# Expert outputs added by one-hot and diagonal products on TensorE, with another order and size of the expert tiles

## What is computed

```python
def hier_moe(h, w_rg, b_rg, w_re, b_re, w_gate, w_up, w_down):
    t = h.reshape(b * s, d)
    p_group = softmax(t @ w_rg + b_rg)
    pg_top, g_top = top_k(p_group, 1)
    p_exp = softmax(einsum('nge,ng->ne', logits_e, g_onehot))
    pe_top, e_top = top_k(p_exp, 2)
    pe_top = pe_top / sum(pe_top)
    combine = one_hot(g) * one_hot(e) * pe_top * pg_top
    for gi in range(4):
        hid = silu(einsum('nd,edf->nef', t, w_gate[gi])) * einsum('nd,edf->nef', t, w_up[gi])
        y = y + einsum('nef,efd->nd', hid * combine[:, gi, :, None], w_down[gi])
# afterwards: x = x + gate(c) * y ; out = rms_norm(x, final_norm)
```

## Time and profile before

| | |
|---|---|
| median of 3 runs | 781.9 us (779.35 to 783.69) |
| the profiled run | 781.9 us, of which the span is 780.0 us |
| busy, share of the span | PE 88%, DVE 41%, ACT 23%, POOL 15% |
| granted TensorE clock, mean | 0.946 of full |
| moved by DMA | 173.62 MB, mean 223 GB/s |

### The profile page before, as it was taken

How to read it: one execution, slowest core, us unless ns; L and a number is a source line. 1 busy time by engine, 2 the same in 40 slices (tenths; PEclk the granted TensorE clock), 3 DMA queues, 4 the chain that set the end, 5 groups by cost and what they waited for, 6 DMA issues and landing times.

```text
span 780.0 us, 9903 instructions
## 1 busy us (share of the span) xinstructions
PE 686.8 (88%) x3851; PEld 401.5 (51%) x3851; DVE 318.2 (41%) x752; ACT 180.0 (23%) x434; POOL 116.7 (15%) x164
## 2 busy tenths in 40 slices
PE   1799899999999999879999985899999999999830
PEld 1674446667666697545654455444444544443210
DVE  3203657856466533786612228350211211202126
ACT  3204215122121121456711141020111211201103
POOL 8700122313032155000000000010000000000030
PEclk9989999999999999899999986999999999999975
DMA  9999003793330300750085047638999999999965
GB/s 332 375 264 364 3 1 108 245 294 109 108 108 1 52 5 7 266 216 2 1 324 108 28 179 280 195 110 349 375 423 413 405 413 409 390 404 410 421 208 201
DMA packets 75475, 173.62 MB, mean 223 GB/s; under 512 B 21954, under 2 KB 38940, under 8 KB 71836
## 3 DMA queue, kind: packets, MB, share of 16 engines
q1 hardware_dynamic: 69520, 157.59, 56.0%
q0 software_dynamic: 2672, 9.44, 3.5%
q10 hardware_dynamic: 3228, 5.84, 2.0%
HBM read 156.59 MB, written 16.26 MB: 222 GB/s over the span
## 4 chain that ended last, share of the span: by engine, by line
PE 76%; DVE 9%; POOL 4%; issue 4%; ACT 3%; DMA 3%; POOLq 0%; ACTq 0%; DVEq 0%
PE ps L1031 14%; PE ps L1153 7%; PE ps L1064 7%; PE ps L2300 7%; PE ps L2267 5%; PE ps L1025 4%; PE ps L1059 2%; PE ps L2378 2%; PE ps L2264 2%; PE ps L2384 2%; DMA expert_rows<-yo 2%; PE ps L2291 2%; POOL lev L1648 2%; PE ps L653 2%; PE ps L2388 2%
## 5 line engine op out<-in xcount | busy, mean ns | idle before, releaser
L1031 PE MATMUL ps<-gu,xgT 128*128 128x512 f32 x256 | 113.0, 600 | 3.6 <-DVE xgT L1110 2.5
L1031 PEld LDWEIGHTS ps<-gu,xgT 128*128 128x128 f32 x256 | 48.6, 192 | 63.2 <-issue 63.2
L2300 PE MATMUL ps<-hT,winr 128*128 128x512 f32 x144 | 72.6, 612 | 0.0
L1540 POOL DMA_INDIRECT xg<-xn_rows,list x15 | 13.9, 928 | 384.7 <-DVE list L1447 185.9
L1153 PE MATMUL ps<-wout,yT 128*128 128x512 f32 x128 | 57.6, 610 | 0.0
L1064 PE MATMUL ps<-dn,hidT 128*128 128x512 f32 x128 | 56.5, 594 | 0.0
L1753 POOL TENSOR_TENSOR cc<-low,lev 128x512 f32<-128x512 f32 x20 | 30.2, 1518 | 129.5 <-DVE low L2087 104.0
L1891 DVE SCALAR_TENSOR_TENSOR acc<-ada,st,acc 128x512 f32<-128x512 f32 x56 | 48.5, 866 | 1.3
L2267 PE MATMUL ps<-hT,wind 128*128 128x512 f32 x96 | 43.4, 605 | 0.0
L1025 PE MATMUL ps<-gu,xgT 128*32 128x256 f32 (+1 forms) x384 | 43.0, 452 | 0.0
L1153 PEld LDWEIGHTS ps<-wout,yT 128*128 128x128 f32 x128 | 24.6, 195 | 30.0 <-issue 30.0
(11 more groups left out here) (433 smaller groups left out, 1046.6 us busy)
## 6 DMA issues: line engine op xcount, KB each, us to landing
dn<-in_w_down SPq DMA_DIRECT2D x16, 2048.0 KB, 23.3
gu<-in_w_gate SPq DMA_DIRECT2D x15, 2048.0 KB, 21.5
gu<-in_w_up SPq DMA_DIRECT2D x15, 2048.0 KB, 26.0
ada<-in_w_ada SPq DMA_DIRECT2D x12, 2048.0 KB, 11.6
expert_rows<-zero SPq DMA_DIRECT2D x12, 512.0 KB, 6.7
expert_rows<-yo ACTq DMA_DIRECT2D x8, 512.0 KB
wout<-in_w_out SPq DMA_DIRECT2D x1, 3072.0 KB, 10.6
x<-in_x SPq DMA_DIRECT2D x2, 1024.0 KB, 6.2
```

What stands on the lines that cost most here:

```text
L1031: ins = nc.tensor.matmul(PS[2 * b + w][:, :], T["xgT"][:, k, :], w_in[:, w, k, :], start=(k == 0), stop=(k == KT - 1))
L2300: ins = t.matmul(bank[:, :], w(k), T["hT"][:, k, :], start=(k == 0), stop=(k == KT - 1))
```

## The change

- Tile sizes are 7 x 128, 5 x 64, 4 x 32, the order is 0, 1, 2, 12, 3, 11, 4, 10, 5, 9, 6, 8, 7, 13, 14, 15, and there are 13 extra tiles.
- Positions 4 and 5 are refilled in quarters too, as the products of positions 1 and 2 go on.
- The last three positions (`on_chip`) are not stored. VectorE writes their 32 rows each to `yc` in SBUF. In the routing it also makes one-hot rows times the weight for them; TensorE turns these at position 4 (`pe_onehot`), ScalarE copies them to `back`. For a token of such an expert the weight of the gathered row is set to zero, and its slot points to a zero row.
- y1 is gathered when the positions up to 11 are stored and G(13) has ended, y2 when position 12 is stored.
- At the end TensorE multiplies y1 and y2 by diagonals of w1 and w2 (`diag1`, `diag2`) and `yc` by `back`, summed in all 8 PSUM banks, 24 products of 128x512 (`pe_back`). VectorE adds the banks to x2.
- Extra tiles stand inside one branch that is not taken when there are none, with a gather and sum of their own.
- The mean and epsilon of two norms move into ScalarE's Sqrt, whose table is loaded ahead of the last norm.

```diff
-SIZES = [128] * 8 + [64] * 4 + [32] * 4
+SIZES = [128] * 7 + [64] * 5 + [32] * 4
+CHIP = 3
...
-                if n == NBUF:
+                if n < 2 * NBUF:
+                    b = n - NBUF
                     for part in range(4):
                         if part < 3:
-                            sp.wait_ge(sem("first_gu_mm"), part + 1)
+                            sp.wait_ge(sem("first_gu_mm"), 3 * b + part + 1)
                         else:
-                            sp.wait_ge(sem("gu_mm"), 1)
+                            sp.wait_ge(sem("gu_mm"), b + 1)
                         ks = slice(2 * part, 2 * part + 2)
                         for w, view in enumerate((wg_v, wu_v)):
-                            sp.dma_start(gu[0][:, w, ks], view[expert[n]][:, ks]).then_inc(sem("gu_in0"), 16)
+                            sp.dma_start(gu[b][:, w, ks], view[expert[n]][:, ks]).then_inc(sem(f"gu_in{b}"), 16)
...
+    def pe_back(pe):
+        pe.wait_ge(sem("routing"), ROUTING["route_i"])
+        pe.wait_ge(sem("exp_out"), 3)
+        pe.wait_ge(sem("diag"), 1)
+        pe.wait_ge(sem("y1_in"), 16 * ST)
+        for i in range(ST):
+            if i == 2:
+                pe.wait_ge(sem("yo_d"), E + 1)
+            for n in range(2):
+                if n:
+                    pe.wait_ge(sem(f"y_in{i}"), 16)
+                for w in range(2):
+                    nc.tensor.matmul(PS[2 * i + w][:, :], T[f"diag{n + 1}"][:, i, :],
+                                     T[f"y{n + 1}"][:, i, w * 512:(w + 1) * 512], start=(n == 0), stop=False)
+            pe.wait_ge(sem("yo_d"), E + 1)
+            for w in range(2):
+                ins = nc.tensor.matmul(PS[2 * i + w][:, :], T["back"][:, i * P:(i + 1) * P],
+                                       T["yc"][:, w * 512:(w + 1) * 512], start=False, stop=True)
+            ins.then_inc(sem("oproj_mm"), 1)
...
+        if on_chip(n):
+            dve.wait_ge(sem("yo_d"), E - CHIP + 1)
+            dve.wait_ge(sem("xg_tr"), E)
+            to = slice(32 * (n - E + CHIP + 1), 32 * (n - E + CHIP + 2))
+            for w in range(4):
+                rows, c = slice(32 * w, 32 * w + 32), slice(256 * w, 256 * w + 256)
+                ins = nc.vector.tensor_tensor(T["yc"][to, c], PS[down_bank(n)][rows, 0:256], T["g2q"][rows, :],
+                                              ALU.mult)
...
         dve_output(dve, E - 1)
+        for i in range(ST):
+            dve.wait_ge(sem("oproj_mm"), ST + i + 1)
+            for w in range(2):
+                x = T["x2"][:, i, w * 512:(w + 1) * 512]
+                ins = v.tensor_tensor(x, PS[2 * i + w][:, :], x, ALU.add)
+            ins.then_inc(sem("x3"), 1)
...
+        extras(dve, n_extra, extra, extra_rows_back)
         dve.wait_ge(sem("fn_in"), 16)
...
-            dve.wait_ge(sem(f"y_in{i}"), 16)
-            v.scalar_tensor_tensor(x, T["y2"][:, i, :], w2[:, i:i + 1], x, ALU.mult, ALU.add).then_inc(sem("x3"), 1)
...
         pool.wait_ge(sem("routing"), ROUTING["slots"])
-        pool.wait_ge(sem("yo_st"), 16 * STORED[E - 1])
+        pool.wait_ge(sem("gu_mm"), E - CHIP + 1)
+        pool.wait_ge(sem("yo_st"), 16 * STORED[E - CHIP - 1])
         for i in range(ST):
             rows_back(0, "y1_in", i)
-        n_extra = extras(pool, extra)
...
-        pool.wait_ge(sem("yo_st"), 16 * STORED[E])
+        pool.wait_ge(sem("yo_st"), 16 * STORED[E - CHIP])
         for i in range(ST):
             rows_back(1, f"y_in{i}", i)
```

More of the change, by code:

```diff
@@ L188, in sbuf_map @@
     o2 = at("r16", o2, [P, ST, E])
+    at("back", o2 + 2 * K, [P, S])
+    at("diag1", o2, [P, ST, P])
     o2 = at("in_row", o2, [P, 2, ST, P])
@@ L1014, in pe_gate_up @@
         w_in = gu[buffer_of(n)]
-        pe.wait_ge(sem(f"gu_in{buffer_of(n)}"), 32 * loads_of(n) + (96 if n >= NBUF and not buffer_of(n) else 0))
+        pe.wait_ge(sem(f"gu_in{buffer_of(n)}"), 32 * loads_of(n) + (96 if n >= NBUF else 0))
         pe.wait_ge(sem("xgT_a"), n + 1)
@@ L1136, in dve_output, with extra_count, extras @@
         ins.then_inc(sem("yo_d"), 1)
-    def extras(eng, body):
+    def extra_count(eng):
         eng.wait_ge(sem("routing"), ROUTING["route_i"])
[L1141 to L1145, removed]
+        return eng.value_load(T["route_i"][0:1, 0:1], min_val=0, max_val=EXTRA)
+    def extras(eng, n_extra, body, last=None):
+        with eng.If(n_extra > 0):
+            for x in range(EXTRA):
+                with eng.If(n_extra > x):
+                    body(x, E + x)
+            if last:
+                last()
     Y_ORDER = (0, 1, 6, 7, 2, 3, 4, 5)
@@ L1252, in extra @@
             pe_down(pe, n)
-        extras(pe, extra)
+        extras(pe, n_extra, extra)
     def act_moe(act):
@@ L1304, in extra @@
             act_hidden(act, n, 0)
+            if n == E:
+                act.wait_ge(sem("yo_zero"), 16 * (EXTRA + 1))
             act_output(act, n)
-        extras(act, extra)
+        extras(act, n_extra, extra, lambda: act.wait_ge(sem("x3"), 2 * ST))
+        a.activation(rden[:, 0:1], one, ACT.Sqrt)
         for i in range(ST):
@@ L1475, in dve_moe @@
         dve.wait_ge(sem("routing"), ROUTING["w12"])
+        slotf, virtual, mine = T["slotf"][:], T["place"][:], T["first"][:]
+        link(v.tensor_scalar(virtual, slotf, 32.0 - CHIP_ROW, None, ALU.add))
+        for n, w in enumerate((w1, w2)):
+            for i in range(ST):
+                ins = v.tensor_scalar(T["in_row"][:, n, i, :], T["row_n"][:], virtual[:, n, i:i + 1], w[:, i:i + 1],
+                                      ALU.is_equal, ALU.mult)
+        link(ins)
+        v.tensor_tensor(T["in_row"][:, 0], T["in_row"][:, 0], T["in_row"][:, 1], ALU.add).then_inc(sem("routing"), 1)
+        link(v.tensor_scalar(mine, slotf, CHIP_ROW - 0.5, None, ALU.is_gt))
+        link(v.scalar_tensor_tensor(virtual, slotf, -float(ZERO_ROW), mine, ALU.add, ALU.mult))
+        link(v.tensor_tensor(slotf, slotf, virtual, ALU.subtract))
+        link(v.tensor_scalar(mine, mine, -1.0, 1.0, ALU.mult, ALU.add))
+        link(v.tensor_tensor(w1, w1, mine[:, 0], ALU.mult))
+        link(v.tensor_tensor(w2, w2, mine[:, 1], ALU.mult))
         swap, move = T["mx"][:], T["mn"][:]
-        link(v.tensor_scalar(t16, order, float(LAST), None, ALU.is_equal))
-        link(v.tensor_tensor(T["s16"][:], T["M1"][:], t16.unsqueeze(1).broadcast_to([P, ST, E]), ALU.mult))
-        link(v.tensor_reduce(swap, T["s16"][:], AX.X, ALU.add))
+        link(v.tensor_scalar(swap, T["slotf"][:, 0, :], MID_ROW - 0.5, None, ALU.is_gt))
         for one_of, two in ((w1, w2), (T["slotf"][:, 0, :], T["slotf"][:, 1, :])):
@@ L1492, in dve_moe @@
         link(v.tensor_scalar(T["rf"][:, 1:1 + EXTRA], T["rf"][:, 1:1 + EXTRA], float(E - 1), None, ALU.min))
-        v.tensor_copy(T["route_i"][:, 0:1 + EXTRA], T["rf"][:, 0:1 + EXTRA]).then_inc(sem("routing"), 1)
+        link(v.tensor_copy(T["route_i"][:, 0:1 + EXTRA], T["rf"][:, 0:1 + EXTRA]))
+        for i in range(ST):
+            ins = v.tensor_scalar(T["diag2"][:, i, :], idf[:], w2[:, i:i + 1], None, ALU.mult)
+        ins.then_inc(sem("routing"), 1)
+        n_extra = extra_count(dve)
         for n in range(1, E):
@@ L1500, in dve_moe @@
                 dve_output(dve, n - 1)
-        dve_output(dve, E - 1)
+            if n == E - 2:
+                v.memset(T["yc"][0:32, :], 0.0)
+            if n == ONEHOT_AT + 1:
+                dve.wait_ge(sem("routing_pe"), ROUTING_PE["list_mm"] + 1)
+                for i in range(ST):
+                    ins = v.tensor_scalar(T["diag1"][:, i, :], idf[:], w1[:, i:i + 1], None, ALU.mult)
+                ins.then_inc(sem("diag"), 1)
+        dve_output(dve, E - 1)
+        for i in range(ST):
+            dve.wait_ge(sem("oproj_mm"), ST + i + 1)
[3 more added lines that the diff above has]
+            ins.then_inc(sem("x3"), 1)
         def extra(x, n):
@@ L1689, in _ @@
         link(g.iota(T["row_i"][:], pattern=[[1, P]], base=0, channel_multiplier=0))
-        edges = [0] + STEPS_DOWN + [E - 1, E, E + EXTRA]
-        runs = [(a, b, (SIZES + [P] * EXTRA)[a]) for a, b in zip(edges, edges[1:])]
+        runs, a = [], 0
+        while a < E + EXTRA:
+            b, step = a + 1, max(1, (TILE_START + [0])[a + 1] - TILE_START[a])
+            while b < E + EXTRA and TILE_START[b] - TILE_START[b - 1] == step:
+                b += 1
+            runs.append((a, b, step))
+            a = b
         for a, b, step in runs:
```

134 lines of the change are left out of this document (88 added, 46 removed).

## The result

The kernel after takes 789.73 us (median of 4 runs, 785.91 to 791.45), the kernel before 781.16 beside it; the ratio is 1.0129, with an interval of 1.0093 to 1.0165 (the two medians alone give 1.011). It is slower, by 8.6 us in the medians. The forecast was 791, in a range of 780 to 796.

What follows compares the result with a forecast made beforehand. The stream of weights was taken to bound the expert stage; 780.0 + 9.7 (D(15) later) + 0.2 (products for gathers and sums) - 0.3 (norm with jump) = 789.6 us, with 1.9 around it written as 791, range 780 to 796.

Steps and rivals of the forecast that it cites:

- The bound: Expert stage: the stream of weights sets the pace; taking products off TensorE alone moves the end by less than 2 us.
- small gains in the stream: Weights before the y gathers: quarter refills gain 1.0 us, 64 fewer rows gathered and stored 1.3; last weights at 741.8 us.
- The schedule by steps: TensorE's start times of gate/up products G(n), by adding a duration per position: G(5) at 582.8 us, G(13) at 710.0.
- The gathers: Gathers of y1 and y2, 4.19 MB, meet the last weights and delay them by their full 12.1 us; dn(15) lands at 753.9.
- The clock: TensorE after idling ahead of G(15): slower matmuls add 1.8 us to 3.6; D(15) was put at 1.9 us.
- TensorE for VectorE: Behind D(15): 24 products, 20.6 us, plus a 1.3 us addition, 21.9 in all, replace 21.7 us of gathers and sums.
- The norm: Final norm: jump 1.0 us, four scalings 6.0, then 3.0 to the span's end, against 10.3 us before.
- The jump: VectorE's branch past the extra tiles' code, ahead of the norm's scalings: 1.0 us, between 0.2 and 2.6 if code is fetched.
- Rival B: End of the stream: weights keep their place and gathers fill in behind, D(15) done at 745.5; time 783 us, chance 0.22.
- C: Expert stream: 416 GB/s is no ceiling, 441 holds, gathers may ride along; time 776 us (782 with full gather delay), chance 0.18.
- D: Tile sizes don't fit the tokens, so an extra tile runs with a second gather; time beyond 825 us, chance 0.02.

Runs made afterwards that it cites:

- the two runs on it: The kernel before with only the new tile sizes (ratio 0.9993), and the kernel before with only positions 4 and 5 refilled in quarters (ratio 0.9989).

## Why the prediction was right

**The bound.** Right: with sizes or quarters by themselves the time cannot be told from the one of before. The small gains in the stream were forecast at 1.3 us (64 rows fewer) and 1.0 us (quarters). In dn(15)'s landing the sizes gave nothing (0.4 us later) and the quarters 1.1; with both, and no gathers ahead of it, it lands 1.0 us earlier than in before, forecast 2.3.

**The schedule by steps.** G(5), G(11), G(12), G(13) were forecast at 582.8, 683.8, 698.6, 710.0 and came at 582.3, 683.3, 698.2, 709.8.

**The gathers.** The mechanism was right, sizes were off. Their price is 9.8 us, not 12.1: the rate of the software queue over a long stretch was the wrong row, and the rate of the whole stream, which gave 10.1, nearly the right one. With the 1.3 us less gained before them, the two errors cancel in part: dn(15) lands 8.8 us later than in before, forecast 9.8. The premise that a loaded queue does not hold the gathers back much was wrong: they took 21.0 us to land instead of 9.7 or 6.2. The weights paid for the bytes all the same. y1 left at 718.9, not 722, and y2 at 726.9, not 734, since the stores landed sooner under this load than the 11.0 us of the earlier trace rows. The landings also split otherwise: gu(15) at 743.3, not 748.8, and dn(15) 9.4 us behind it, not 5.1; the software queue's share of 33.9% in 735 to 745 us shows that the gathers still ran while dn(15) was on its way. So D(15) had to wait for its own weights and not for the chain from G(15).

**The clock.** G(15) took 6.2 us where 5.4 was forecast (granted clock 0.58 in 743.34 to 749.60 us), and D(15) 3.19 where 1.9 was (0.59 in 752.82 to 756.00): one wait was priced, two came. D(15)'s end came at 756.0, forecast 757.6, and that it came so near is in part luck. gu(15) was 5.5 us early, and by the forecast's own steps from there (5.4, 1.5 and 1.9 us) D(15) would have ended at 752.1; the wait for dn(15) and the second drop of the clock, neither of them in the forecast, took 3.9 us back.

**TensorE for VectorE.** 20.6 us forecast, 20.9 measured; x3 complete 22.1 us after D(15), forecast 21.9. What it replaced took 21.7 us in before and 20.4 in the two runs on it, so the exchange cost 0.4 to 1.7 us.

**The norm.** The jump was put at 1.0 us between 0.2 and 2.6; it cost nothing that shows. VectorE's additions take 1.29 us, and the branch may have been taken beneath them; that was not tested. The stall that the Trainium skill states for a branch out of the loaded pages (page "Runtime: NRT & Kernel Launch", section on instruction fetch) does not show here; whether the target lay in the loaded pages is not known. The rest was 8.7 us, forecast 9.0.

**Sum.** From the start of G(4), the profile of the kernel after is 7.0 us longer: +8.3 until D(15) ends, +0.4 until x3 is complete, -1.7 in the norm. Forecast: +9.7, +0.2, -0.3, in all 9.6. The medians differ by 8.6 us, so the time came within 1.3 us of the forecast, and the profiled pair would have put it 2.6 us below. Rival B (gathers fill in behind the weights) is refuted by the landing of dn(15); C by 397 to 399 GB/s from 580 to 700 us. Of D nothing was seen: there are 15 gathers of rows again.

## What to carry to other kernels

When a stream of loads keeps the DMA engines full to the end, a gather moved ahead of its last load costs its bytes at the stream's rate (here 9.8 us). Moved behind the last load it left the end where it was (222.3 against 222.0 us). Work moved to another engine is worth what that engine would otherwise idle: here VectorE idled ahead of the last expert, while TensorE's new products could only stand behind it. Before an order is changed at such an end, write down for each engine what stands behind the last landing.

## What the runs showed of the hardware

Gathers of 8 or 64 of 128 partitions, amid the stream, left the DMA engines as busy (share 1.03 and 1.01), but the engines moved 321 and 295 GB/s in the window in which they moved 427 with full gathers. The cause stays open; other row counts and other places in the stream were not tried.
